# Grams of four levels in one block of the TensorE stream, and the product with the values one step later

## What is computed

```python
def step(state, inp):
    qx, kx, lfx, vx = inp
    b = jnp.cumsum(lfx, axis=2)
    rel = b[:, :, :, None, :] - b[:, :, None, :, :]
    decay = jnp.exp(jnp.where(causal, rel, -jnp.inf))
    scores = jnp.einsum('bhtk,bhsk,bhtsk->bhts', qx, kx, decay)
    o = (jnp.einsum('bhts,bhsv->bhtv', scores, vx)
         + jnp.einsum('bhtk,bhkv->bhtv', qx * jnp.exp(b), state))
    ...
o = o_f + o_b                      # one scan per direction, summed
o = o * lax.rsqrt(jnp.mean(o * o, axis=-1, keepdims=True) + NORM_EPS)
```

## Time and profile before

| | us |
|---|---|
| median of 3 runs | 2150.7 (2150.51 to 2152.18) |
| the profiled execution | 2152.27 |
| its span, first to last instruction | 2150.5 |
| PE busy | 2133.7 (99% of the span) |
| DVE busy | 1557.7 (72%) |
| POOL busy | 1249.4 (58%) |
| ACT busy | 1062.7 (49%) |
| mean granted TensorE clock | 0.998 |

### The profile page before, as it was taken

How to read it: one execution, slowest core, us unless ns; L and a number is a source line. 1 busy time by engine, 2 the same in 40 slices (tenths; PEclk the granted TensorE clock), 3 DMA queues, 4 the chain that set the end, 5 groups by cost and what they waited for, 6 DMA issues and landing times.

```text
span 2150.5 us, 28852 instructions
## 1 busy us (share of the span) xinstructions
PE 2133.7 (99%) x11598; PEld 1768.1 (82%) x11598; DVE 1557.7 (72%) x2192; ACT 1062.7 (49%) x1040; POOL 1249.4 (58%) x583
## 2 busy tenths in 40 slices
PE   9999999999999999999999999999999999999998
PEld 7888888888888887888888888888888888878887
DVE  7872789898876786555388737898898767865653
ACT  6444444446566654434454434345566565644442
POOL 4455544336785867666534555443366867666664
PEclk9999999999999999999999999999999999999999
DMA  8555545345455454655565555453554544546554
GB/s 323 194 195 196 176 160 193 140 185 184 176 180 184 167 182 171 255 195 190 185 222 190 192 195 176 159 193 137 193 180 175 179 181 170 187 166 250 191 191 151
DMA packets 59764, 403.86 MB, mean 188 GB/s; under 512 B 6768, under 2 KB 6896, under 8 KB 12272
## 3 DMA queue, kind: packets, MB, share of 16 engines
q1 hardware_dynamic: 59488, 401.49, 52.0%
q10 hardware_dynamic: 144, 0.52, 0.1%
HBM read 397.80 MB, written 4.19 MB: 187 GB/s over the span
## 4 chain that ended last, share of the span: by engine, by line
PE 75%; DVE 13%; POOL 5%; issue 3%; ACT 3%; DMA 1%; DVEq 0%; POOLq 0%; ACTq 0%
PE acc L1282 70%; PE side L1282 4%; DVE w_lo L490 4%; DVE arena L951 2%; POOL w_lo L490 2%; POOL arena L618 1%; ACT w_hi L487 1%; DVE arena L1107 1%; POOL arena L615 1%; DVE wide L951 1%; POOL arena L616 1%; DMA raw<-w_stream 1%; DVE arena L1102 1%; DVE arena L1076 0%; DVE arena L1067 0%
## 5 line engine op out<-in xcount | busy, mean ns | idle before, releaser
L490 POOL TENSOR_TENSOR w_lo<-raw,w_hi 128x768 fp32r<-128x768 f32 x367 | 1019.4, 2778 | 855.4 <-ACT w_hi L487 844.3
L487 ACT ACTIVATE w_hi<-raw 128x2048 fp32r<-128x2048 f32 x366 | 701.0, 1915 | 873.3 <-PE acc L1282 855.0
L490 DVE TENSOR_TENSOR w_lo<-raw,w_hi 128x1280 fp32r<-128x1280 f32 (+1 forms) x371 | 613.7, 1656 | 511.1 <-ACT w_hi L487 508.0
L1282 PE MATMUL acc<-w_hi,xT_hi 128*128 128x512 f32 x2112 | 654.6, 393 | 0.3 <-DVE w_hi L996 0.2
L1282 PE MATMUL acc<-w_hi,xT_lo 128*128 128x512 f32 x2112 | 648.3, 390 | 0.0
L1282 PE MATMUL acc<-w_lo,xT_hi 128*128 128x512 f32 x2112 | 526.3, 391 | 0.0
L1282 PEld LDWEIGHTS acc<-w_hi,xT_lo 128*128 128x128 f32 x2112 | 396.7, 188 | 83.8 <-DVE xT_lo L451 0.2
L1282 PEld LDWEIGHTS acc<-w_lo,xT_hi 128*128 128x128 f32 x2112 | 393.9, 188 | 82.0 <-issue 0.2
L1282 PEld LDWEIGHTS acc<-w_hi,xT_hi 128*128 128x128 f32 x2112 | 393.1, 188 | 79.9 <-DVE w_hi L996 0.4
L951 DVE STREAM_TRANSPOSE arena<-stage 32x256 f32<-32x256 f32 (+1 forms) x480 | 204.8, 427 | 7.0
L1107 DVE TENSOR_TENSOR arena<-arena 128x512 f32<-128x512 f32 x64 | 84.9, 1326 | 30.7 <-ACT arena L855 30.7
(11 more groups left out here) (147 smaller groups left out, 1940.3 us busy)
## 6 DMA issues: line engine op xcount, KB each, us to landing
raw<-w_stream SPq DMA_DIRECT2D x366, 1024.0 KB, 4.8
x_out<-arena SPq DMA_DIRECT2D x16, 256.0 KB, 3.0
arena<-x_turned_in SPq DMA_DIRECT2D x4, 514.0 KB, 7.6
arena<-x_in SPq DMA_DIRECT2D x2, 1024.0 KB, 14.7
arena<-x_in SPq DMA_DIRECT2D x4, 512.0 KB, 6.2
wide<-post_in SPq DMA_DIRECT2D x2, 1024.0 KB, 6.9
arena<-x_out SPq DMA_DIRECT2D x4, 512.0 KB, 5.7
raw<-w_stream SPq DMA_DIRECT2D x3, 512.0 KB, 7.3
```

What stands on the lines that cost most here:

```text
L487: return act.activation(w_hi[:, g % ROUNDED, :], raw[:, g % LANDING, :], ACT.Copy)
L490: return eng.tensor_tensor(w_lo[:, g % LANDING, cols], raw[:, g % LANDING, cols], w_hi[:, g % ROUNDED, cols].bitcast(F32), ALU.subtract)
L1282: return pe.matmul(out, a, b, start=start, stop=stop)
```

## The change

Grams stand in three blocks: (-1, 0, 1, 2) at +3, (3, 4, 5, 6) at +7, (7) at +8. Keys get 5 buffers, decayed queries 4, and grams 4 PSUM banks, two of them in `side[1]`. VectorE keeps grams -1 and 0 at +3, 1 at +4, 2 at +5, 3 and 4 at +7, and 5, 6 and 7 at +8, now behind L1107 of the step. The product with the values moves from behind `lo_pass` of +8 to between `hi_pass` and `lo_pass` of +9, its followers one step later, and so do the last turn of branch c (`TURN_C[3]`) and the loads that hang on it. A new tensor `extra` of 6 KB per partition holds the added buffers, and the space for software-made DMA descriptors is set to 8192 bytes.

```diff
+BLOCK_AT = {2: (-3, -2, -1, 0), 6: (-3, -2, -1, 0), 7: (0,)}
+KEEPS_AT = {3: (-1, 0), 4: (1,), 5: (2,), 7: (3, 4), 8: (5, 6, 7)}
-TURN_C = [Z_A_END + 1, Z_A_END + 3, REC[3] + 5, REC[3] + FIRST_LEVEL + 11]
+TURN_C = [Z_A_END + 1, Z_A_END + 3, REC[3] + 5, REC[3] + FIRST_LEVEL + 12]
...
+        extra = sb("extra", [P, 3, 512])
...
-            return [(u, l + i) for u, l in last if l in (0, 2, 4, 6, 7) for i in ((0,) if l == 7 else (-1, 0))]
+            return [(u, l + i) for u, l in last if l in BLOCK_AT for i in BLOCK_AT[l]]
...
-            return (EQ[:, 1], EQ[:, 2], wide[:, 512:1024])[(l + 1) % 3]
+            return (EQ[:, 1], EQ[:, 2], wide[:, 512:1024], wide[:, 1540:2052], extra[:, 0])[(l + 1) % 5]
...
-            return S_off_flat if l % 2 == 0 else EQ[:, 3]
+            return (S_off_flat, EQ[:, 3], extra[:, 1], extra[:, 2])[l % 4]
+
+        def gram_bank(l):
+
+            n = (l + 1) % 4
+            return side[n // 2][:, n % 2 * 512:n % 2 * 512 + 512]
...
-                            if s == REC[u] + FIRST_LEVEL + 9:
+                            if s == REC[u] + FIRST_LEVEL + 10:
...
-                                    if l >= 2:
-                                        act.wait_ge(S.grams, (LEVELS + 1) * u + l - 1)
+                                    if l >= 4:
+                                        act.wait_ge(S.grams, (LEVELS + 1) * u + l - 3)
...
-                            if 0 <= l < LEVELS + 1:
+                            if 0 <= l < LEVELS:
                                 if l == 0 and u:
                                     dve.wait_ge(S.rec_out, u)
...
+                                if l >= 4:
+                                    dve.wait_ge(S.grams, nine + l - 2)
+                                dve.wait_ge(S.decays, LEVELS * u + l + 1)
+                                dve.tensor_tensor(decayed_q(l), q, EQ[:, 0], ALU.mult).then_inc(S.mixed, 1)
+                            for k in KEEPS_AT.get(l, ()):
+                                dve.wait_ge(S.grams, nine + k + 2)
+                                src = gram_bank(k).rearrange("p (b t) -> p b t", t=P)
...
-                        if n >= 2:
-                            pe.wait_ge(S.kept, n - 1)
+                        if l >= 3:
+                            pe.wait_ge(S.kept, n - 3)
+                        elif u:
+                            pe.wait_ge(S.kept, (LEVELS + 1) * u)
...
+                        if l == 1 and u:
+                            pe.wait_ge(S.rec_y, u)
+                        dst = gram_bank(l)
...
+                        if s == REC[u] + FIRST_LEVEL + 9:
+                            pe.wait_ge(S.kept, (LEVELS + 1) * (u + 1))
...
                         level_grams(s)
+                        rec_outs(s)
                         lo_pass(s, [0, 1]).then_inc(pe_step, 1)
...
-                            if d == FIRST_LEVEL + 8:
-                                pe.wait_ge(S.kept, nine + LEVELS + 1)
...
-    nc = bacc.Bacc("TRN2", target_bir_lowering=False, num_devices=1)
+    nc = bacc.Bacc("TRN2", target_bir_lowering=False, num_devices=1, dynamic_dma_scratch_size=8192)
```

More of the change, by code:

```diff
@@ L856, in _ @@
                                                ACT.Exp).then_inc(S.decays, 1)
-                            if d == FIRST_LEVEL + 9:
+                            if d == FIRST_LEVEL + 10:
                                 act.wait_ge(S.rec_out, u + 1)
@@ L1108, in _ @@
-                            if d == FIRST_LEVEL + 8:
-                                dve.wait_ge(S.grams, nine + LEVELS + 1)
-                                dve.tensor_copy(S_off, side[0][:, (nine + LEVELS) % 2 * 512:(nine + LEVELS) % 2 * 512 + 512]
-                                                .rearrange("p (b t) -> p b t", t=P)).then_inc(S.kept, 1)
-                            if d == FIRST_LEVEL + 10:
+                                if l >= 4:
+                                    dve.wait_ge(S.grams, nine + l - 2)
@@ new lines, in _ @@
+                                dve.wait_ge(S.decays, LEVELS * u + l + 1)
[3 more added lines that the diff above has]
+                                src = gram_bank(k).rearrange("p (b t) -> p b t", t=P)
+                                if k == -1:
+                                    ins = dve.tensor_copy(S_diag, src)
+                                elif k == LEVELS - 1:
+                                    ins = dve.tensor_copy(S_off, src)
+                                else:
+                                    dve.wait_ge(S.kept, nine + k + 1)
+                                    ins = dve.copy_predicated(S_diag, lmasks[:, k:k + 1, :].broadcast_to([P, 4, P]), src)
+                                ins.then_inc(S.kept, 1)
@@ L1113, in _ @@
+                            if d == FIRST_LEVEL + 11:
                                 dve.wait_ge(S.rec_rstd_ready, u + 1)
@@ L1389, in level_grams @@
                         pe.wait_ge(S.mixed, n + 1)
-                        if n >= 2:
-                            pe.wait_ge(S.kept, n - 1)
+                        if l >= 3:
+                            pe.wait_ge(S.kept, n - 3)
+                        elif u:
+                            pe.wait_ge(S.kept, (LEVELS + 1) * u)
                         if n == 0:
                             pe.wait_ge(S.branch_lo, 3)
-                        dst = side[0][:, n % 2 * 512:n % 2 * 512 + 512]
+                        if l == 1 and u:
+                            pe.wait_ge(S.rec_y, u)
+                        dst = gram_bank(l)
                         qq = q if l < 0 else decayed_q(l)
@@ L1407, in level_grams, with rec_outs @@
                         ins.then_inc(S.grams, 1)
+                def rec_outs(s):
+                    for u in range(4):
+                        _, _, v, _, _, j = rec_views(u)
+                        if s == REC[u] + FIRST_LEVEL + 9:
+                            pe.wait_ge(S.kept, (LEVELS + 1) * (u + 1))
+                            evacuated(pe, S, CHUNKS.index(("c_v", u // 2, KT)))
+                            if u:
+                                pe.wait_ge(S.rec_y, u)
+                            for h in range(2):
+                                for tt in range(MT):
+                                    i = h * MT + tt
+                                    o = side[1][:, i * P:(i + 1) * P]
+                                    mm(o, S_diag[:, i], v[:, tt, (j + h) * HD:(j + h + 1) * HD], stop=False)
+                                    ins = mm(o, S_off[:, h * MT + 1 - tt], v[:, 1 - tt, (j + h) * HD:(j + h + 1) * HD],
+                                             start=False)
+                            ins.then_inc(S.rec_out, 1)
                 pe.wait_ge(warm_ready, 1)
@@ L1473, in _ @@
                                 ins.then_inc(S.attended, 1)
-                        for u in range(4):
-                            d = s - REC[u]
-                            _, _, v, _, _, j = rec_views(u)
-                            nine = (LEVELS + 1) * u
-                            if d == FIRST_LEVEL + 8:
-                                pe.wait_ge(S.kept, nine + LEVELS + 1)
-                                evacuated(pe, S, CHUNKS.index(("c_v", u // 2, KT)))
-                                if u:
-                                    pe.wait_ge(S.rec_y, u)
-                                for h in range(2):
-                                    for tt in range(MT):
-                                        i = h * MT + tt
-                                        o = side[1][:, i * P:(i + 1) * P]
-                                        mm(o, S_diag[:, i], v[:, tt, (j + h) * HD:(j + h + 1) * HD], stop=False)
-                                        ins = mm(o, S_off[:, h * MT + 1 - tt], v[:, 1 - tt, (j + h) * HD:(j + h + 1) * HD],
-                                                 start=False)
-                                ins.then_inc(S.rec_out, 1)
                     last_two_steps()
```

13 lines of the change are left out of this document (removed).

## The result

The changed kernel takes **2155.4 us** (median of 19 runs, 2154.05 to 2156.55), the kernel before 2152.2 us in the same session (19 runs). The ratio is 1.0016, with a 95% interval of 1.001 to 1.0022. The prediction was 2135.4 us and faster; the kernel became slower by 0.16%. That is less than the 0.2% that the prediction gave as what a measurement can tell, but the interval rules out that it became faster. The profiled execution took 2155.26 us, 3.0 us more than that of before.

What follows compares the result with a forecast made beforehand. PE, busy for 99% of the span, bounds the kernel. Merges in units 0 to 2 4.7, unit 2's wait 1.0, unit 3 1.6, products 8.0: together 15.3 us, from 2150.7 to 2135.4 us; range about 2131.5 to 2143.5.

Steps and rivals of the forecast that it cites:

- The price of a block: PE's cost for each block of grams, however many levels stand in it: 0.39 us, saved at each merge.
- Rival 3 (long bursts starve): Merged blocks' second half cannot be fed at 17 ns a matmul; 48 us lost, 2183 us; chance 0.03.
- The product a step later: Steps +8 and +9: the product's wait and the slow clock behind it go; 8.0 us, bounds 6.5 and 8.1.
- the 5.5 us of the new place: The product stands behind a whole `hi_pass`, some 5.5 us later on PE, so its wait should be gone.
- Unit 0: the 0.87 us of slack just cover 0.78: At gram 6, the queries' slack covers PE's earlier arrival from two merges; full gain, no wait.
- Unit 3: The chain of levels binds up to gram 6; PE gains 0.29 us plus 0.5, 1.6 us in two layers.
- The step that failed: Unit 2, gram 6: two keeps leave the front of L1107, so the old wait goes; 1.0 us in two layers.
- POOL and DVE as makers of `w_lo`: They make it two steps ahead and get no new work; no cost, or 0.73 us per keep without that cover.
- a new wait that eats everything: A new wait, with no place given, takes the whole gain; chance 0.03, shared with the rest.
- Rival 1: Queries come no earlier in any unit, merged blocks only meet waits, only products pay; 2142.7 us; chance 0.11.
- The low end of its range: Merges at 0.42 us, unit 3's chain faster by 1.7 us in both layers, products 8.1: about 2131.5 us.

Runs made afterwards that it cites:

- experiment 1: The kernel before with only the product and its followers one step later; 2143.8 us, ratio 0.9957.
- experiment 2: The changed kernel with the product back behind `lo_pass` of +8 and its followers back one step; 2178.5 us, ratio 1.0118.
- experiment 8: The changed kernel with grams -1 and 0 not kept in unit 2 of each layer; 2149.5 us, ratio 0.999.
- experiment 3: The changed kernel with grams -1 to 2 not kept in unit 2 of each layer; 2142.2 us, ratio 0.995.
- experiment 7: The kernel before with the product and followers one step later and ScalarE's split moved behind the level's exponentials; 2149.2 us, ratio 0.9987.
- experiment 12: The changed kernel without GpSimd's three sums of level 5 in unit 2 of both layers; 2144.8 us, ratio 0.9969.
- experiment 13: The changed kernel without GpSimd's sums of levels 5 and 6 in unit 2; 2147.7 us, ratio 0.9981.
- experiment 6: The changed kernel with 20 matmuls of zeros on PE ahead of its wait for gram 6's queries in unit 2; 2150.9 us, ratio 0.9996.
- Experiment 11: The changed kernel with second block, gram 7, product and followers one step later, and ScalarE's split behind the level's exponentials; 2138.3 us, ratio 0.9939.
- experiment 10: The changed kernel with 10 matmuls of zeros on PE ahead of unit 2's chain; 2160.2 us, ratio 1.0042.

## Why the prediction was wrong

- **The price of a block: right, slightly high.** Four blocks of a unit cost 3.94 us before (what their steps take beyond plain steps) and the two cost 3.22 now, 0.36 us for each merge where 0.39 was taken. 5.8 us in the 8 units.
- **Rival 3 (long bursts starve): refuted.** The third level starts 0.29 to 0.34 us behind the second and the fourth 0.29 us behind the third, against 0.27 in the first half: less than 0.1 us a block, where 0.96 would have decided against the change. The 62 ns that the Trainium skill gives for a matmul handled by the sequencer's firmware (TensorE: Matmul & The Clock Gate, Part 1) would have shown as 1 us a level; the trace disagrees.
- **The product a step later: right.** 8.1 us in the difference of the traces (without gram 7's new wait in unit 3), 8.3 us in experiment 1. The trust in the 5.5 us of the new place was well founded, and experiment 2 shows that it is needed.
- **"Unit 0: the 0.87 us of slack just cover 0.78": wrong by a little.** A wait of 0.65 us is left in each layer, since the queries are ready at 556.72 + 1.11 = 557.83, 0.64 us later than before. The keep that was thought gone from the front of L1107 has a successor, keep 2, which now stands ahead of level 6, and L498 before it takes 2.47 us where L490 took 1.88; no run here took either away alone in unit 0.
- **Unit 3: 1 us a layer too high,** as the old wait of 0.70 us became one of 1.0 at the first block and 0.5 each at gram 6 and gram 7.
- **The step that failed: "DVE works without a pause there, and two of its six keeps ahead of this L1107 move behind it, 2 x 0.73 = 1.5 us", so that unit 2's wait "goes as well".** The keeps were counted, and not where they stood. Those of the first steps had stood among pauses and had cost nothing, so that their leaving gave nothing back. Keeps -1 and 0 arrived at +3, ahead of a stretch where VectorE has no pause, and cost it 1.4 us (1.7 in experiment 8). A gain of 0.5 us became a wait of 4.9 us: 0.4 that the queries were late before, 0.6 that PE wants them sooner, and 3.9 by which VectorE fell behind. These 3.9 are 1.4 for the two keeps, 0.3 and 2.4 for instructions that took longer, less 0.2 for one that took less. Order acts twice here, by the keeps' own length and by what it brings together: without all four keeps the wait was 0.5 us and the instructions had their old lengths (experiment 3).
- **"POOL and DVE as makers of `w_lo`. They get no new work ... No cost": wrong.** No work was added, but a shift of a keep or two changed which instructions of the two engines meet, and VectorE's took 2.4 us longer in unit 2 (experiments 3, 7, 12 and 13). This is the larger part of the failed step, and no term of the sum stood for it.
- **The clock was left out.** 4.1 us of the result are PE at 1.2 GHz behind the two waits (experiment 6). A row of before showed this price already, the 0.61 of the earlier trace rows; it was counted as a gain where a wait goes, and not as a risk where one might come.
- **Chances.** 0.03 for "a new wait that eats everything" was too little. The forecast gave PE's slack in unit 2 as exhausted, and VectorE there as saturated; both spoke for a larger chance. Rival 1 came nearest in kind. It had the queries come no earlier than before, and so it was in unit 2 for level 5; those of level 6 came even 2.2 us later (ready at 737.96 against 735.75).
- **Two numbers of the forecast.** The low end of its range adds up to 2132.6 by its own terms (12 merges at 0.42, unit 2's 1.0, twice 0.29 + 1.7 in unit 3, and 8.1), not 2131.5. And it started from 2150.7, the median of three runs; the median of 19 is 2152.2. Neither changes the verdict.

The sum: blocks -5.8, product -8.1, old waits at the levels -3.2, new waits with their clock +19.2, the late tile +0.7, rounding 0.2: +3.0 us.

Experiment 11 shows that the forecast's terms were there to be had. With both the blocks' own time and the product's, and no new wait, the units gained 16.3 us where 15.3 were forecast. Part of this are the old waits of unit 3, which the forecast didn't count in full.

## What to carry to other kernels

When a change moves small work from one step of a helper to another, ask for each piece whether it left a pause or a stretch without one, and beside which instructions of the other engines it shifts what stands behind it; a count of instructions ahead of the critical one is not enough. A wait of TensorE can cost more than itself, by what follows at half the clock: here 4.9 us of wait cost 6.9. And an instruction's duration that is read beside a busy GpSimd is not a property of the instruction: look for its shortest and longest form in the trace (here 0.87 to 3.38 us), and give the difference as a bound when the order changes.

## What the runs showed of the hardware

- **VectorE and GpSimd take turns by whole instructions.** Alone, the split takes 0.87 us (two instructions) and VectorE's `w_lo` 1.49 us. Where GpSimd's instruction was first, VectorE's lasted to about its end and then its own time: 2.68 and 3.07 us for `w_lo`, and 3.37 for the split, whose two instructions met two of GpSimd's. Where VectorE's was first, GpSimd's paid. The kernel before shows that case, beside its L490 at 732.68 (GpSimd's timeline), against the same sum when it was not held up in the changed kernel:

```profile
733.01 2.19 POOL L618 TENSOR_TENSOR arena<-arena 128x512 f32<-128x512 f32 x1
```

```profile
733.20 1.06 POOL L626 TENSOR_TENSOR arena<-arena 128x512 f32<-128x512 f32 x1
```

  The Trainium skill has the rule (SBUF — State Buffer, Who interferes with whom): an instruction of VectorE with two inputs in SBUF and one of GpSimd that reads SBUF contend for a port that they share, whoever starts first holds it for the whole instruction, and the other is blocked, not slowed. The trace agrees, with these numbers. Where the recorded starts are 20 ns apart they don't tell who won (experiment 10).
- **VectorE's keeps are not held up:** the copies take 0.67 to 0.69 us and the masked ones 0.72 to 0.76 in both traces, beside a busy GpSimd too. They read the gram from PSUM; that this is why is not shown.
- **A wait of 4.8 us and the stretch behind it:** the granted clock was 0.50 for 6.8 us, and the step lost 2.0 us by it. In experiment 12 the wait was 1.6 us, and the clock stayed at 1.00. The kernel before shows that the length of the wait doesn't settle it: ahead of the product of unit 3 PE waited 1.88 us in both layers; in the first the clock stayed at 1.00, in the second it fell.
- **64 loads and matmuls of 32 columns in a row** run nearly as fast as 32: 17 ns each in the first half of the block, 18 to 21 in the second.
